# A convolution, an output projection and expert 0's rows in another order, in a hybrid block on one Trainium2 core

## What is computed

```python
h = rms_norm(x, norm_mix[l])
(cb, cc, cx, aq, ak, av, gq, gk, gv, gr, gz) = jnp.split(h @ w_in[l], split_points, axis=-1)
y_conv = short_conv(cb, cc, cx, conv_w[l], conv_b[l])    # b * (bias + sum_j w_j * (c * x)[t - 2 + j])
...
y_attn = moba_attention(q, k, v, rel_bias_table)
y_gla = gla(gq, gk, gv, gr, gz, w_gla_alpha[l], b_gla_alpha[l], gla_out_norm[l])
merged = jnp.zeros_like(x)
for n, y_b in enumerate((y_conv, y_attn, y_gla)):
    merged = merged + jax.nn.sigmoid(h @ w_merge_gate[l, n]) * (y_b @ w_branch[l, n])
x = x + merged @ w_out[l]
h2 = rms_norm(x, norm_ffn[l])
x = x + hier_moe(h2, ...)    # silu(h2 @ w_g[e]) * (h2 @ w_u[e]) @ w_d[e] for the two experts e of each token
```

## Time and profile before

| | |
|---|---|
| median of 3 runs | 726.35 us (726.0 to 728.36) |
| the profiled execution | 727.15 us |
| its span, first to last instruction | 724.8 us |
| TensorE busy | 588.5 us (81%) |
| VectorE busy | 302.1 us (42%) |
| ScalarE busy | 192.5 us (27%) |
| GpSimd busy | 25.2 us (3%) |
| moved by DMA | 247.73 MB, mean 342 GB/s |
| clock granted to TensorE, mean | 0.891 |

### The profile page before, as it was taken

The page is one execution under the profiler, slowest core; times in us unless marked ns, Lnnn a source line. Parts: engine busy times, 40 slices in busy tenths (PEclk is TensorE's granted clock), DMA queues, the critical chain, the costliest instruction groups (busy, mean ns, idle before and its releaser), DMA issues.

```text
span 724.8 us, 15347 instructions
## 1 busy us (share of the span) xinstructions
PE 588.5 (81%) x6592; PEld 413.2 (57%) x6592; DVE 302.1 (42%) x620; ACT 192.5 (27%) x332; POOL 25.2 (3%) x55
## 2 busy tenths in 40 slices
PE   3999999989999997997667765778586876876584
PEld 3977899989999795554333332334243433443342
DVE  5475886885464935444031132112311122212312
ACT  4484455364444624211001010011000110011101
POOL 8002100000000000000000000000000000000000
PEclk9999999999999999999688798778867697788978
DMA  9974565634569749999999999999999999999993
GB/s 265 359 264 134 176 191 163 204 122 139 210 224 422 284 166 415 408 426 424 427 429 424 428 426 426 427 425 428 426 426 427 426 426 426 426 427 428 424 417 157
DMA packets 38531, 247.73 MB, mean 342 GB/s; under 512 B 4296, under 2 KB 4384, under 8 KB 24384
## 3 DMA queue, kind: packets, MB, share of 16 engines
q1 hardware_dynamic: 37008, 245.44, 83.8%
q0 software_dynamic: 912, 1.25, 1.0%
q10 hardware_dynamic: 544, 0.06, 0.1%
HBM read 245.67 MB, written 1.06 MB: 340 GB/s over the span
## 4 chain that ended last, share of the span: by engine, by line
PE 49%; DMA 44%; DVE 3%; issue 1%; ACT 1%; another core or an unknown queue 1%; SPq 0%; DVEq 0%; ACTq 0%
DMA wide<-in_w_expert_up 38%; PE ps L1321 8%; PE ps L1013 6%; PE ps L1014 6%; PE ps L1015 6%; DMA wide<-in_w_expert_down 5%; PE ps L1356 3%; PE ps L986 3%; PE ps L988 3%; PE ps L987 3%; PE ps L1281 2%; DMA ring<-in_w_in 2%; PE ps L1368 1%; PE ps L1336 1%; DVE ring_lo L1441 1%
## 5 line engine op out<-in xcount | busy, mean ns | idle before, releaser
L1321 PE MATMUL ps<-wide,xe 128*32 128x256 f32 x2048 | 164.0, 474 | 109.0 <-DMA wide<-in_w_expert_up 107.1
L1321 PEld LDWEIGHTS ps<-wide,xe 128*32 128x32 f32 x2048 | 76.9, 132 | 177.0 <-issue 133.3
L1812 DVE TENSOR_TENSOR xe<-ps,g_ffn 128x256 f32<-128x256 f32 x32 | 13.6, 425 | 262.2 <-PE ps L1290 262.2
L1441 DVE TENSOR_TENSOR ring_lo<-ring,w_hi 128x1024 fp32r<-128x1024 f32 x76 | 91.6, 1223 | 46.1 <-ACT w_hi L700 45.8
L700 ACT ACTIVATE w_hi<-ring 128x1024 fp32r<-128x1024 f32 x76 | 79.1, 1057 | 59.2 <-PE ps L1015 38.2
L1013 PE MATMUL ps<-hT_hi,w_hi 128*128 128x256 f32 x320 | 90.3, 282 | 5.0 <-issue 2.8
L1014 PE MATMUL ps<-hT_lo,w_hi 128*128 128x256 f32 x320 | 89.4, 279 | 0.0
L1015 PE MATMUL ps<-hT_hi,ring_lo 128*128 128x256 f32 x320 | 89.3, 279 | 0.0
L1356 PE MATMUL ps<-wide,he 128*32 128x256 f32 x1024 | 63.2, 386 | 2.7 <-DMA wide<-in_w_expert_down 2.7
L1013 PEld LDWEIGHTS ps<-hT_hi,w_hi 128*128 128x128 f32 x320 | 60.8, 190 | 6.3 <-issue 3.3
L909 ACT ACTIVATE he<-ps 128x128 f32<-128x128 f32 x32 | 8.9, 278 | 207.0 <-PE ps L1336 203.5
(11 more groups left out here) (272 smaller groups left out, 770.5 us busy)
## 6 DMA issues: line engine op xcount, KB each, us to landing
wide<-in_w_expert_gate SPq DMA_DIRECT2D x27, 2048.0 KB, 45.3
wide<-in_w_expert_up SPq DMA_DIRECT2D x27, 2048.0 KB, 48.4
wide<-in_w_expert_down SPq DMA_DIRECT2D x27, 2048.0 KB, 41.0
ring<-in_w_in SPq DMA_DIRECT2D x9, 2048.0 KB, 13.2
ring<-in_w_merge_gate SPq DMA_DIRECT2D x6, 2048.0 KB, 9.6
wide<-in_w_expert_gate SPq DMA_DIRECT2D x10, 1024.0 KB, 12.2
wide<-in_w_expert_up SPq DMA_DIRECT2D x10, 1024.0 KB, 11.7
wide<-in_w_expert_down SPq DMA_DIRECT2D x9, 1024.0 KB, 12.2
```

The lines of the kernel that those rows point to most:

```text
L1321: ins = t_.matmul(ps[q * WIN:(q + 1) * WIN, b, 0:QW], xe[b][:, k % 2, k // 2, :], w, start=(k == 0), stop=(k == KD - 1))
L1441: v.tensor_tensor(piece(ring_lo, g, c), piece(ring, g, c), by_row(out_hi[g == 19][c]).bitcast(F32), ALU.subtract).then_inc(wpre_lo, 1)
```

## The change

Three places are written in another order, the third with other operations too.

1. **Convolution.** Both `conv_in` stand at head 4 ahead of `row_max(4)`, `conv_taps(0)` and `(1)` behind `row_max(4)` and `(5)` instead of `(5)` and `(6)`, `conv_out(0)` behind `row_max(6)` and `conv_out(1)` ahead of `row_max(7)`.
2. **Output projection.** Rows 0 to 3 of out_proj(1, 0) stand between rows 0 to 3 and 4 to 7 of out_proj(0, 0). Of its rows 4 to 7, two stand ahead of the transposes of tile 0 and two behind them.
3. **Expert 0.** `pick_w` of expert 0 is, for each tile, (place number == the token's position in expert 0's column) x (1 if expert 0 is one of its two): one small addition and two operations, ahead of the slots. `choose(0, 1)`, expert 1's choice, and `rows_in(0, 0)` stand ahead of the count, the weights and the table of places.

```diff
--- before.py
+++ after.py
@@ -1222,11 +1222,13 @@
                 if ks[-1] == KD - 1:
                     ins.then_inc(router_mm, 1)
 
-            out_proj(0, 0)
+            out_proj(0, 0, range(0, 4))
+            out_proj(1, 0, range(0, 4))
+            out_proj(0, 0, range(4, KD))
             out_proj(0, 1)
-            out_proj(1, 0, range(0, 4))
+            out_proj(1, 0, range(4, 6))
             turn_x1(0, range(KD), 2)
-            out_proj(1, 0, range(4, KD))
+            out_proj(1, 0, range(6, KD))
             pe.wait_ge(router_ready, 1)
             route(0, range(0, 4), 1)
             route(0, range(4, KD), 2)
@@ -1654,17 +1656,16 @@
                 low_pre(7 + (h - 1) // 2, (0, 1) if h % 2 else (2, 3))
                 if h == 4:
                     conv_in(0)
-                if h == 7:
-                    conv_out(0)
+                    conv_in(1)
                 if h >= 4 and h % 2 == 0:
                     pair_out(h // 2 - 2)
-                row_max(h)
-                if h == 4:
-                    conv_in(1)
-                if h in (5, 6):
-                    conv_taps(h - 5)
                 if h == 7:
                     conv_out(1)
+                row_max(h)
+                if h in (4, 5):
+                    conv_taps(h - 4)
+                if h == 6:
+                    conv_out(0)
             prob_scale(NH - 1)
             low_pre(10, (2, 3))
             pair_out(2)
@@ -1787,8 +1788,13 @@
             dve.sem_inc(back_ready, 1)
             dve.sem_inc(now_ready, 1)
             dve.wait_ge(assign_ready, 4)
+            link(v.tensor_tensor(stat[:, 44:46].unsqueeze(2), eh[:, :, 0, 0:1], eh[:, :, 1, 0:1], ALU.add))
             dve.wait_ge(pos_mm, 1)
             spot = ps[:, 3, 0:2 * NE].rearrange("p (t e) -> p t e", e=NE)
+            for tt in range(TT):
+                ins = v.scalar_tensor_tensor(out=pick_w[0][:, tt, :], in0=iota_w[:, :], scalar=spot[:, tt, 0:1],
+                                             in1=stat[:, 44 + tt:45 + tt].broadcast_to([P, WIN]), op0=ALU.is_equal, op1=ALU.mult)
+            ins.then_inc(chosen_ready, 1)
             for k in range(TOPK):
                 ins = v.tensor_tensor(hits[:, :, k, :], eh[:, :, k, :], spot, ALU.mult)
             link(ins)
@@ -1813,11 +1819,10 @@
                                 g_ffn[:, :].rearrange("p (q j) -> p j q", q=NQ).unsqueeze(3).broadcast_to([P, 2, NQ, WIN]),
                                 ALU.mult).then_inc(xe_ready, 1)
 
-            v.tensor_tensor(both, places, flat_slots, ALU.is_equal).then_inc(same_ready, 1)
-            dve.wait_ge(same_ready, 1)
-            v.tensor_tensor(pick_w[0][:, :, :], same[:, :, 0, :], same[:, :, 1, :], ALU.add).then_inc(chosen_ready, 1)
-
+            dve.sem_inc(same_ready, 1)
             dve.wait_ge(table_ready, 1)
+            choose(0, 1)
+            rows_in(0, 0)
             link(v.tensor_reduce(cntr[:, 0:1], tab[0:1, 1, :], AX_X, ALU.max))
             link(v.tensor_scalar(cntr[:, 1:2], cntr[:, 0:1], float(WIN), 1.0, ALU.is_gt, ALU.add))
             for r in range(2, MAXWIN):
@@ -1839,7 +1844,6 @@
                                         in1=inside[:, :, :], op0=ALU.add, op1=ALU.mult))
             v.tensor_scalar(flat(place_tab[:, :, :]), flat(place_tab[:, :, :]), -1.0, None,
                             ALU.add).then_inc(place_ready, 1)
-            rows_in(0, 0)
             passes = dve.alloc_register("passes_dve")
 
             def gated(p, e):
@@ -1879,7 +1883,7 @@
                     dve.wait_ge(moved, p)
                     choose(NE * p, 0)
                     rows_in(NE * p, 0)
-                choose(NE * p, 1)
+                    choose(NE * p, 1)
                 dve.wait_ge(place_ready, 1)
                 dve.wait_ge(back_ready, NE * p + 1)
                 v.tensor_copy(place_now[:, :], flat(place_tab[:, :, :])[:, bass.ds(p * NE, NE)]).then_inc(now_ready, 1)
```

## The result

| | before | after |
|---|---|---|
| median, same rounds | 727.0 us (726.0 to 728.36, 4 runs) | 719.58 us (719.03 to 720.77, 4 runs) |
| ratio, 95% interval | | 0.9891 (0.9875 to 0.9908) |
| the profiled execution, its span | 727.15, 724.8 | 720.02, 717.8 |
| mean of all executions of this study | 727.13 (74) | 720.34 (10) |

The change makes the kernel faster, by 6.8 us from mean to mean (two standard errors give that 0.7 either way). In the four rounds of the first row alone the medians lie 7.4 us apart; six later executions of the changed kernel were 1.0 slower on average than these four, so I go by all executions. The forecast, 5.5 us down to 720.8, had the direction and most of the mechanism; the size was 1.3 too small.

The account below looks back on a forecast made before the run. TensorE was taken to set the pace until the expert weights stream, then the stream, with a fixed tail. Savings 2.9 + 2.1 + 0.5 = 5.5 us from 726.35 gave 720.8 us, range 719.2 to 723.8.

Parts of the forecast that it names:

- Convolution, 2.9: TensorE's wait ahead of gate projection 10 goes; the piece starts at 151.3 to 151.4 instead of 154.28, 2.9 us.
- The working on VectorE: Summing VectorE's operations from 131.54, 19.6 us, frees the second bank for gate projection 10 at 151.2.
- That rival, 732: Without the rest ahead of gate projection 10, TensorE's clock falls to 1.2 GHz under load: slower, 732 us; chance 0.03.
- Output projection, 2.1: Both TensorE waits in out_proj(0, 0) go: 2.1 us, or 1.6 if only idle time is counted.
- The hole, 0.5: Unit 22, issued 2.0 us earlier, closes the weight stream's loss at 289 to 292: 0 to 0.9, taken as 0.5 us.
- The steps on expert 0: Earlier choice and rows_in(0, 0) start gate_up(0) 2.0 us earlier; new choice operations cost 0.3 to 0.6; count runs beside gate_up(0).
- The rival of the clock staying up in expert 0: In gate_up(0) the clock stays up, saving up to 1.6 us of TensorE; whole hole closes, 720.4 us; chance 0.2.
- Half a wait: The wait at 154 is only shortened, a 1.4 us slip in heads 5 to 7 passed on: 722.2 us; chance 0.12.
- a new wait: Another wait takes the convolution's whole gain and the hole stays; only the output projection's gain remains: 724.5 us; chance 0.07.
- no gap of TensorE above 0.3 us between 131 and 164: Sign for the convolution: a TensorE wait over 0.3 us between 131 and 164 would prove that step wrong.

Follow-up runs that it names:

- outproj_only: The kernel before with only the output projection's new order: 725.98 us median, ratio 0.9981 to the kernel before.
- expert0_only: The kernel before with only expert 0's new order and choice: 727.52 us median, ratio 0.9999 to the kernel before.
- tail_busy: The full change with filler products in TensorE's waits for the last expert's down weights: 721.48 us median, ratio 0.9931 to the kernel before.
- rest_filled8: The kernel before with eight unused filler products in TensorE's wait ahead of gate projection 10: 726.26 us median, ratio 0.9998 to the kernel before.
- before_3: The kernel before, unchanged, in another profiled execution: span 724.3 us.
- tile1_early: The full change with out_proj(1, 0) finished ahead of out_proj(0, 1), unit 12 behind the second finished piece: 718.9 us median, again 719.6.

## Why the prediction was right and wrong

**Convolution, 2.9: the step that failed.** The working on VectorE held to 0.1 us: the second bank free at 151.18, the piece at 151.35, no new wait, passage 3.04 shorter than in the profile on which the sum stood. What failed is that the wait was priced at its own length. The sum took the distance from 151.3 or 151.4 to 154.28 out of one execution and called it the gain, 2.9 us; behind that same wait the clock falls in six executions of seven, 1.65 us on average over all seven. The profile held a hint: in the earlier trace rows the clock stood at 0.53 behind shorter waits ahead of expert 0, so the wait of 2.81 us with a full clock behind it was the thing to be surprised by. The forecast asked only the opposite, whether the rest protects the clock. That rival, 732, is refuted: thirteen profiles without the rest have a granted clock of 1.00 there. The Trainium skill (TensorE: Matmul & The Clock Gate, "What's actually happening") says that the point at which the clock of a starting kernel rises varies from run to run. The traces here show as much in the middle of a kernel, for the fall behind this wait and the rise that ends it: they cost nothing to 2.94 us from one execution to another.

**Output projection, 2.1: right.** The last issue of SyncE ahead of unit 12 is that of unit 10, in the profile before:

```profile
246.42 0.33 SPq L529 DMA_DIRECT2D wide<-in_w_expert_gate  x1
```

and at 243.50 after. From it to unit 12 it takes 16.61 before and 14.45 after, 2.16 less, and 14.46 in `outproj_only`. The times of `outproj_only` alone (1.3, plus or minus 1.2) would not have shown it so well. No wait appeared at turn_x1(0) or route(0).

**The hole, 0.5: wrong in the other direction.** It was real in the first profile (0.8 to 0.9, as worked out), and it closed. But it comes only when the clock falls in `gate_up(0)`, in one of the thirteen profiles without part 3 (one of five of the kernel before), so on average the term is 0.1 to 0.2 us at most, and `expert0_only` shows none; I put it at zero. The steps on expert 0 themselves held, each at its time: 2.15 us of TensorE's time won ahead of gate_up(0), the choice at 0.42 (0.3 to 0.6), the count beside `gate_up(0)`; TensorE only waits later for the stream. Unit 22 came at 279.94, not near 281.8, since gate_up(0) took 1.93 us and not 3.47.

**The rival of the clock staying up in expert 0** (720.4) did come about, but it is also the usual state of the kernel before, and so not what brings the gain. The number came near the truth for a wrong reason. So did the forecast's own 720.8, against a mean of 720.3: the gain was 1.3 too small, and the 726.35 from which it was taken was 0.8 under the mean of all executions before. That is luck. Half a wait and a new wait: refuted, no gap of TensorE above 0.3 us between 131 and 164.

**The sum with the right sizes:** 3.04 + 1.65 + 2.16 + 0 = 6.85 us, against 6.8 measured; each has 0.7 either way, so that they meet this closely is chance. From unit 12 on the kernels agree: to the end of the last wait for weights it is 448.8 to 449.5 us in sixteen profiles, with and without the change (in `tail_busy` filler stands in that wait, and the start of the products behind it is taken). The others are before's first, 450.3 with its hole, and the two kernels whose holes were made.

**Not settled:** the upper half of `rest_filled8`'s times, and the rest of the spread. The start of the program (1.5 us between the earliest and the latest) and the tail (1.3) explain part of it.

## What to carry to other kernels

A wait of a few microseconds on TensorE can cost its length and, in part of the executions, the work behind it at half the clock, as the one of 2.8 us did here: price it from several profiles, or add the lower level's time as a bound, and look at the count of matmuls and the granted clock behind each wait, not at the busy share. Where a queue is ahead of its consumer, find the limit from which lateness costs (here 24.5 to 25.0 us behind unit 12); inside it an engine's gain is worth nothing. A hole seen in one profile can be that execution's own; distances between two issues of the same queue separate such effects to 0.01 us where medians of ten runs leave half a microsecond.

## What the hardware did that I had not expected

- Behind the same wait of 2.80 us the clock fell or stayed, and where it fell the cost differed by a factor of two (1.32, 1.35, 1.58, 1.66, 2.72, 2.94 us). Nor does it fall at a fixed point: in `before_3` it fell inside the wait, which ended at 153.77 (granted 0.79 in 152 to 154), in `expert0_only` only when TensorE was at work again, from 153.68 on (1.00 in 152 to 154, 0.76 in 154 to 156). Shorter waits, 1.47 us ahead of `gate_up(0)` in the kernels without part 3, had a fall behind them in one profile out of thirteen.
- From 150 to unit 12 the rest repeats almost exactly: the passage is 12.52 or 12.53 in nine profiles of six kernels, from its end to the issue of unit 10 it is 80.61 to 80.63 in all twenty, and from there to unit 12 16.60 to 16.64 or, in the new order, 14.44 to 14.46 (8.00 in `tile1_early`).
- A filler product of float32 operands, 128 x 128 x 256, is two instructions and takes 0.41 us, where the matmuls that the profile prints with the same shape, in the projections, start 0.11 apart.
